# One transformer-like program on one core: four pieces of work put in another order on ScalarE and VectorE

## The chip, the core and the metric

The program runs on one core of one Trainium2 chip. Its engines work side by side, each on its own list of instructions, and wait for each other on semaphores: TensorE (PE) multiplies matrices, VectorE (DVE) and ScalarE (ACT) work element by element, SyncE (SP) starts the transfers from memory. The metric is the device time of one execution in microseconds (us). Shorter is better.

## The reference, cut to what matters

Two blocks follow each other on 256 tokens of width 1024, all in float32. The first has a modulated norm, a gated linear attention with a pooling branch, and 32 experts of which each token uses two. The second is where most of the change lies:

```
h = h + 0.5 * swiglu(rms_norm(h, ffn1_norm), ...)
u = rms_norm(h, mix_norm);  z = u @ w_in
(aq, ak, av, iq, ik, iw, rq, rk, rv, rg, ga, gb) = split(z)
aq, ak, iq, ik, rq, rk = rope(...)                       # rotation by position
y_a = dsa_attention(aq, ak, av, iq, ik, iw, n_sel=64)    # 64 best keys of an index score, then softmax
y_r = group_norm_heads(retention(rq, rk, rv), ret_gn) * silu(rg)
h = h + (sigmoid(ga) * (y_a @ w_branch_a) + sigmoid(gb) * (y_r @ w_branch_b)) @ w_out
h = h + 0.5 * swiglu(rms_norm(h, ffn2_norm), ...)
gate = sigmoid(rms_norm(h, ple_norm) @ w_ple_gate);  h = h + gate * (p @ w_ple_proj)
```

Of the first block the change touches the norm `x * rsqrt(mean(x*x) + 1e-6)` at its very start, beside the modulation `silu(c) @ w_ada`.

## The kernel before

Activations lie feature by token: a tile has 128 features on the partitions and 256 tokens beside each other, 8 tiles for the width. Weights come in chunks of 1 MB (128 x 2048), one DMA each, issued by SyncE into a ring of `raw` buffers; a buffer is loaded again when its last reader has given it back. Every product of an activation with a weight is made of three matmuls (`mm3`): both sides are split into a high part in a rounded format (`wh`, `hh`, `yh`) and a low part that holds the rest (`wl`, `hl`, `yl`). For the weights ACT copies half a chunk into `wh` (L1253, 128x1024) and DVE subtracts that from `raw` into `wl` (L1828). There are six slots of each, so both engines can be some halves ahead of PE. `ahead(name, i)` splits up to two chunks behind the named one, `through(name, i)` up to it, `done(...)` waits until PE has used it.

No scheduler orders the work. `tensor_program`, `scalar_program` and `vector_program` are written out by hand, and each engine runs its list in that order. A wait holds up everything behind it on its engine. PSUM has eight banks, given out to named jobs in the order of the PE list; `evicted(name)` waits until a bank has been read.

Four places matter:

- The start (ACT, L1296 to L1312). ACT squares the 8 tiles of `x` (L1299) for PE, which sums them with a matrix of ones; `root("statx", ...)` takes the square root, for which ACT must load another function table. `ada_row(1)` copies a row of `silu(c) @ w_ada` out of PSUM once PE has made it. Then come the squares of the context (L1309), which PE sums next. VectorE inverts the root (L1852), scales `x` and then the context, and both engines form the first inputs of the matmuls with `w1ak` (L1322 to L1328).
- The index queries (ACT L1669 to L1675, DVE L2468 to L2474). `shifted` copies the halves that the rotation swaps (L1601), `rope_rest` does the rotation (L2383 to L2389). PE is busy there with `w2rq`.
- The selection (DVE, `pick`, L2410 and L2492 to L2501). Eight rounds, in each of which for both halves of the queries the eight largest scores are found (L2413) and struck out (L2414). In between lie the splits for the weights `w2rv` and what follows, and `ret_scores(h)` (L2424), which multiplies the retention scores by their decays; PE's `ret_values(h)` waits for it.
- The four gates `rg` of the retention and the softmax of the attention (ACT L1711 to L1729, DVE L2517 to L2530). For each h there are `ahead("w2rg", h)`; for h = 0 and 1 the variance and mean of the last group norms (`ret_var`, `ret_mean`); the gate (`Silu`, and the product L2527, split by L1728 and L1848); and `attention(h)`. On DVE `attention(n)` masks and scales the logits (L2452), takes their maximum (L2455) and negates it (L2456), waits for ACT's two exponentials (L1659), and divides by the sum (L2458, L2460). `Sqrt`, `Silu` and `Exp` each need their own table on ACT. PE works in this order: `rg` h, then for n = h the transposes of softmax n-1 (L1106, `att_turn`, waits for L2460) and the logits of n (`att_probs`); at odd n from 3 on the attention values of two earlier ones go ahead (`att_values`). The same goes on for n = 4 to 7 beside `w2ga`.

Of the kernel before, what the change touches and what calls it, by code (L numbers as in the profile page):

```python
# [61 lines left out]
def program(nc, D, out):  # L62
# [8 lines left out]
    with cx:  # L71
# [16 lines left out]
        def S(name):  # L88
            return sems[name]

        def nth(name, n):
            return sems[name], base[name] + n
# [1146 lines left out]
        def scalar_program(a):  # L1239
# [56 lines left out]
            for k in range(8):  # L1296
# [2 lines left out]
                a.activation(SQ[k % 2][:, :], XT[:, k, :], ACT.Square).then_inc(S("sqx"), 1)  # L1299
                if k == 3:  # L1300
                    ada_row(0)
            ada_row(1)
            a.wait_ge(*nth("eps", 2))
            root("statx", "sqx_used", 8)
            a.wait_ge(*nth("d_ct", 16))
            for k in range(8):
                if k >= 2:
# [358 lines left out]
            for k in range(8):  # L1666
                a.wait_ge(*nth("hn_t", k + 1))
                a.activation(H1[:, k, :], TN[k % 2][:, :], ACT.Copy).then_inc(S("hn_h"), 1)
            through("w2rq", 0)  # L1669
            evicted(a, ("iq", 0))  # L1670
            shifted(0, TR[0], 2, 0)
            through("w2rq", 1)
            evicted(a, ("iq", 1))
            shifted(1, TR[1], 2, 0)
            rope_in_twice(2, "ik", ("w2ik", 0), TR[0], 8)  # L1675
# [35 lines left out]
            for h in range(4):  # L1711
                lin("w2rg", h)
                if h == 0:
                    ret_var(2)
                    ret_mean(3)
                    v2 = bank("av")[:, 0:128].rearrange("p (a c) -> p a c", a=2)
                    a.wait_ge(*nth("av_t", 1))
                    a.activation(AV[:, :, 0:64], v2, ACT.Copy)
                    copy_out("av", AV[:, :, 64:128], v2)
                elif h == 1:  # L1720
                    ret_var(3)
                if h < 2:
                    a.wait_ge(*nth("rope", 9 + h))
                else:
                    a.wait_ge(*nth("sgy", h - 1))
                copy_out(("rg", h), TR[h % 2], two(bank(("rg", h))), ACT.Silu)
                a.wait_ge(*nth("sgy", h + 1))
                a.activation(YH[:, 2 * h:2 * h + 2, :], YN[:, 2 * h:2 * h + 2, :], ACT.Copy).then_inc(S("rg_h"), 1)  # L1728
                attention(h)  # L1729
            for j in range(4):  # L1730
                lin("w2ga", j)
                a.wait_ge(*nth("rv_mm", 4))
# [83 lines left out]
        def vector_program(v):  # L1816
# [621 lines left out]
            def attention(n):  # L2438
# [6 lines left out]
                        t = v.tensor_tensor(YLA[p, hp, :], b[p, s * 256:s * 256 + 256], YHA[p, hp, :].bitcast(f32), ALU.subtract)  # L2445
                    t.then_inc(copied(("atv", hp)), 1)
                if n < 8:
                    a, P, M, Z = n % 2, P2[n % 2], NM[n % 2], SS[n % 2]
                    v.wait_ge(*nth("at_mm", 2 * n + 2))
                    if n >= 2:  # L2450
                        v.wait_ge(*nth("at_tr", n - 1))
                    v.scalar_tensor_tensor(P, two(bank(("atp", n))), 0.125, MB[:, a, :].unsqueeze(1).broadcast_to([128, 2, 256]), ALU.mult,  # L2452
                                           ALU.add).then_inc(copied(("atp", n)), 1)
                    evicted(v, ("atp", n))
                    chain(v.tensor_reduce(M[:, 0:2].unsqueeze(2), P, AX.X, ALU.max))  # L2455
                    v.tensor_scalar(M[:, 2:4], M[:, 0:2], -1.0, None, ALU.mult).then_inc(S("at_m"), 1)  # L2456
                    v.wait_ge(*nth("at_e", 2 * n + 2))
                    chain(v.reciprocal(Z[:, 2:4], Z[:, 0:2]))  # L2458
                    for s in range(2):
                        t = v.tensor_scalar(P[:, s, :], P[:, s, :], Z[:, 2 + s:3 + s], None, ALU.mult)  # L2460
                    t.then_inc(S("at_d"), 1)
# [6 lines left out]
            through("w2rq", 0)  # L2468
            rope_scaled(0, ("iq", 0), ("w2iq", 0), TR[0])
            rope_scaled(1, ("iq", 1), ("w2iq", 1), TR[1])  # L2470
            rope_rest(0, ("iq", 0), TR[0], 2, 0, IQ[:, 0:2, :])
            through("w2rq", 1)
            rope_rest(1, ("iq", 1), TR[1], 2, 0, IQ[:, 2:4, :])
            rope_rest(2, "ik", TR[0], 1, 0, IK.unsqueeze(1))  # L2474
            through("w2rk", 0)
# [13 lines left out]
            for p0, p1, a, c in ((0, 64, 0, 64), (64, 128, 0, 128), (0, 64, 1, 192)):  # L2489
                step(v.memset(SCO[p0:p1, a, c:256], -1e30))  # L2490
            prev()
            pick(0, 2)  # L2492
            ahead("w2rv", 0)
            pick(2, 4)
            ahead("w2rv", 1)
            ret_scores(0)
            pick(4, 6)
            ahead("w2rv", 2)
            ret_scores(1)
            pick(6, 8)  # L2500
            v.tensor_scalar(MB, WK, -3e38, -1e30, ALU.is_gt, ALU.mult).then_inc(S("ix_sel"), 1)  # L2501
            ahead("w2rv", 3)
            ret_mean(0)
            ret_scores(2)
            ahead("w2aq", 0)
            ret_var(0)
            ret_mean(1)
# [8 lines left out]
            v.wait_ge(*nth("ix_sel", 1))  # L2516
            for h in range(4):  # L2517
                ahead("w2rg", h)
                if h == 0:
                    ret_var(2)  # L2520
                    ret_mean(3)
                elif h == 1:
                    ret_var(3)
                Y2 = YN[:, 2 * h:2 * h + 2, :]
                evicted(v, ("rg", h))
                v.wait_ge(*nth("yn", h + 1))
                v.tensor_tensor(Y2, Y2, TR[h % 2], ALU.mult).then_inc(S("sgy"), 1)  # L2527
                v.wait_ge(*nth("rg_h", h + 1))
                low(YL[:, 2 * h:2 * h + 2, :], Y2, YH[:, 2 * h:2 * h + 2, :], "rg_l")
                attention(h)  # L2530
            for j in range(4):
                ahead("w2ga", j)
                attention(4 + j)
            for n, j in MERGE:
                ahead(n, j)
                if n == "w2gb" and j < 2:
# [276 lines left out]
```

## Time and profile before

| | us |
|---|---|
| median of 3 runs | 1164.95 |
| lowest and highest | 1160.52, 1165.49 |
| profiled execution, its own time | 1163.78 |
| its span | 1161.9 |
| PE busy (share of the span) | 1108.9 (95%) |
| DVE busy | 708.9 (61%) |
| ACT busy | 519.0 (45%) |

The span is the time from the first to the last instruction in the trace; 1.9 us of the execution lie around it. A busy PE is not a PE at its peak: the granted clock of TensorE has two levels, 1.2 and 2.4 GHz, and is shown as 0.5 and 1.0 of full speed; its mean over the span is 0.982. In the timeline a row gives the start in us from the span's start, the time it took, engine, line, operation, tile out of tile in, the count, and in brackets the idle time ahead of it with what ended it.

### The profile page before, as it was taken

How to read it: one execution, taken by the hardware profiler on the slowest of the kernel's cores; microseconds unless marked ns; L12 is line 12 of the kernel's file. 1: busy time of each engine (PE TensorE's matmuls, PEld its weight loads, DVE VectorE, ACT ScalarE, POOL GpSimd, SP SyncE). 2: the span in 40 equal slices, each digit the busy share in tenths (PEclk: the TensorE clock that was granted, in tenths of full speed). 3: DMA queues.
4: the chain of work that ended last, by engine and by line, in shares of the span. 5: the costliest groups of instructions: out<-in, count | busy, mean ns of one | idle time of the engine just before them, and what ended most of it. 6: DMA issues, size and time to landing. Idle time of an engine off the chain costs nothing.

```text
span 1161.9 us, 19096 instructions
## 1 busy us (share of the span) xinstructions
PE 1108.9 (95%) x7978; PEld 942.7 (81%) x7978; DVE 708.9 (61%) x1125; ACT 519.0 (45%) x797; POOL 0.2 (0%) x4
## 2 busy tenths in 40 slices
PE   5999999899999999999999999989999999999997
PEld 3789888545555554999999988987889999999997
DVE  1889868423332334786865689877646775655567
ACT  2773333211111113754444576368844554443455
POOL 0000000000000000000000000000000000000000
PEclk9999999899999999999999999998999999999998
DMA  9955627999999947465554423532246545445321
GB/s 384 357 190 215 245 78 294 382 421 421 417 403 409 411 195 321 144 242 188 208 183 156 180 84 118 181 109 91 92 145 227 182 182 207 184 153 217 127 94 37
DMA packets 38154, 257.74 MB, mean 222 GB/s; under 512 B 4368, under 2 KB 5264, under 8 KB 7856
## 3 DMA queue, kind: packets, MB, share of 16 engines
q1 hardware_dynamic: 36720, 252.38, 56.6%
q10 hardware_dynamic: 1344, 4.08, 0.9%
q8 instruction: 66, 1.08, 0.4%
q14 instruction: 24, 0.20, 0.0%
HBM read 255.39 MB, written 1.05 MB: 221 GB/s over the span
## 4 chain that ended last, share of the span: by engine, by line
PE 71%; DVE 9%; ACT 3%; issue 2%; DVEq 0%; ACTq 0%
PE bank L536 70%; DVE wl L1828 2%; ACT wh L1253 1%; DVE xt L1878 1%; DVE rstd L1852 1%; DVE hl L1895 1%; PE bank L922 0%; DVE acc L1890 0%; PE bank L1106 0%; PE bank L880 0%; DVE tn L1910 0%; DVE arena L2046 0%; ACT arena L1601 0%; DVE acc L2085 0%; DVE raw L1867 0%
## 5 line engine op out<-in xcount | busy, mean ns | idle before, releaser
L536 PE MATMUL bank<-hh,wh 128*128 128x256 f32 (+2 forms) x1256 | 364.3, 290 | 5.4 <-DVE wl L1828 3.4
L536 PE MATMUL bank<-hl,wh 128*128 128x256 f32 (+2 forms) x1256 | 360.0, 287 | 0.0
L536 PE MATMUL bank<-hh,wl 128*128 128x256 f32 (+2 forms) x1256 | 359.9, 287 | 0.0
L1828 DVE TENSOR_TENSOR wl<-raw,wh 128x1024 fp32r<-128x1024 f32 (+4 forms) x238 | 267.7, 1164 | 80.6 <-ACT wh L1253 76.8
L1253 ACT ACTIVATE wh<-raw 128x1024 fp32r<-128x1024 f32 (+4 forms) x238 | 227.9, 1003 | 71.4 <-PE bank L536 71.2
L536 PEld LDWEIGHTS bank<-hh,wh 128*128 128x128 f32 (+1 forms) x1256 | 242.5, 193 | 14.2 <-issue 9.5
L536 PEld LDWEIGHTS bank<-hl,wh 128*128 128x128 f32 (+1 forms) x1256 | 242.5, 193 | 1.0
L536 PEld LDWEIGHTS bank<-hh,wl 128*128 128x128 f32 (+1 forms) x1256 | 242.5, 193 | 0.9
L536 PE MATMUL bank<-yh,wh 128*128 128x256 f32 x512 | 146.6, 286 | 2.2 <-DVE yl L2445 1.7
L536 PE MATMUL bank<-yl,wh 128*128 128x256 f32 x512 | 145.4, 284 | 0.0
L536 PE MATMUL bank<-yh,wl 128*128 128x256 f32 x512 | 145.4, 284 | 0.0
L536 PEld LDWEIGHTS bank<-yh,wh 128*128 128x128 f32 x512 | 98.5, 192 | 3.7 <-issue 2.6
L536 PE MATMUL bank<-arena 64*128 64x256 f32 (+6 forms) x404 | 92.8, 408 | 6.5 <-DVE arena L2142 3.3
L536 PEld LDWEIGHTS bank<-yl,wh 128*128 128x128 f32 x512 | 98.7, 193 | 0.3 <-issue 0.2
L536 PEld LDWEIGHTS bank<-yh,wl 128*128 128x128 f32 x512 | 98.7, 193 | 0.0
L536 PE MATMUL bank<-raw,xg 128*64 128x512 f32 (+1 forms) x352 | 82.5, 567 | 0.1
L536 PEld LDWEIGHTS bank<-arena 64*128 64x128 f32 (+3 forms) x404 | 53.8, 181 | 32.1 <-issue 18.6
L2221 DVE SCALAR_TENSOR_TENSOR arena<-arena,bank 128x256 f32<-128x256 f32 x16 | 7.7, 481 | 106.1 <-ACT arena L1484 106.1
L1263 ACT ACTIVATE arena<-bank 128x512 f32<-128x512 f32 (+4 forms) x79 | 40.4, 532 | 69.3 <-PE bank L536 65.0
L536 PEld LDWEIGHTS bank<-raw,xg 128*64 128x64 f32 (+1 forms) x352 | 28.0, 142 | 45.6 <-issue 45.3
L1484 ACT ACTIVATE arena<-bank 128x256 f32<-128x256 f32 x16 | 6.1, 384 | 108.7 <-PE bank L536 108.7
L536 PE MATMUL bank<-raw,arena 128*64 128x512 f32 (+1 forms) x240 | 50.4, 549 | 1.1 <-DVE yl L2212 1.1
(275 smaller groups left out, 1405.1 us busy)
## 6 DMA issues: line engine op xcount, KB each, us to landing
raw<-in_gu SPq DMA_DIRECT2D x40, 1024.0 KB, 11.4
arena<-in_gu SPq DMA_DIRECT2D x24, 1024.0 KB, 10.4
raw<-in_gd SPq DMA_DIRECT2D x22, 1024.0 KB, 9.0
raw<-in_w_adt SPq DMA_DIRECT2D x14, 1024.0 KB, 6.1
raw<-in_f1g SPq DMA_DIRECT2D x11, 1024.0 KB, 4.8
raw<-in_f1d SPq DMA_DIRECT2D x11, 1024.0 KB, 5.5
raw<-in_f2g SPq DMA_DIRECT2D x11, 1024.0 KB, 4.9
raw<-in_f2u SPq DMA_DIRECT2D x11, 1024.0 KB, 4.9
```

What stands on the lines that cost most here:

```text
L536: return pe.matmul(o, l, m, start=start, stop=stop, skip_group_check=True)
L1253: a.activation(WH[slot_of[U]][:, 0:n], src, ACT.Copy).then_inc(S("wh"), 1)
L1263: a.activation(dst, src, fn).then_inc(copied(name), 1)
L1484: a.activation(SLT[p % 2], bank(("gu", p))[:, 0:256], ACT.Silu).then_inc(S("g_s"), 1)
L1828: v.tensor_tensor(WL[slot_of[U]][:, 0:n], src, WH[slot_of[U]][:, 0:n].bitcast(f32), ALU.subtract).then_inc(S("wl"), 1)
L1852: step(v.reciprocal(RS[:, :], RS[:, :]))
L1878: t = v.scalar_tensor_tensor(XT[:, k, :], b, s, XT[:, k, :], ALU.mult, ALU.add)
L1895: v.scalar_tensor_tensor(L[:, k, :], XT[:, k, :], gain[:, k:k + 1], H[:, k, :].bitcast(f32), ALU.mult, ALU.subtract).then_inc(S(sem), 1)
L2221: v.scalar_tensor_tensor(HSL[p % 2], SLT[p % 2], GC[:, p:p + 1], bank(("gu", p))[:, 256:512], ALU.mult, ALU.mult).then_inc(copied(("gu", p ...
```

## The change

Nothing is added or removed; instructions are put in another order on ACT and DVE. PE's, SyncE's and GpSimd's lists stay as they are.

- Start: `root("statx", ...)` goes ahead of `ada_row(1)` on ACT.
- Index queries: both splits for `w2rq` chunk 1 go ahead, on ACT ahead of the first `shifted`, on DVE ahead of the first `rope_rest`.
- Selection: the rounds, in portions of 2, 2, 2 and 2 between the splits before, are now taken in portions of 1, 2, 2, 1 and 2; the last two rounds and the mask `MB` come behind `ret_mean(0)` and `ret_scores(2)`.
- Gates: on ACT `attention(h)` goes ahead of the gate's `Silu`, and `ret_mean(3)` behind `attention(0)`. On DVE `attention(h)` is cut in two. The first part (mask, maximum, negation) goes ahead of `ret_var` and `ret_mean`, the second (`attention_scaled`: reciprocal and product) ahead of the gate's product.

```diff
@@ scalar_program
-            ada_row(1)
             a.wait_ge(*nth("eps", 2))
             root("statx", "sqx_used", 8)
+            ada_row(1)
@@
             through("w2rq", 0)
+            through("w2rq", 1)
             evicted(a, ("iq", 0))
             shifted(0, TR[0], 2, 0)
-            through("w2rq", 1)
             evicted(a, ("iq", 1))
@@
                 if h == 0:
                     ret_var(2)
-                    ret_mean(3)
                     v2 = bank("av")[:, 0:128].rearrange("p (a c) -> p a c", a=2)
...
                 elif h == 1:
                     ret_var(3)
+                attention(h)
+                if h == 0:
+                    ret_mean(3)
...
                 a.activation(YH[:, 2 * h:2 * h + 2, :], YN[:, 2 * h:2 * h + 2, :], ACT.Copy).then_inc(S("rg_h"), 1)
-                attention(h)
@@ vector_program
                     v.tensor_scalar(M[:, 2:4], M[:, 0:2], -1.0, None, ALU.mult).then_inc(S("at_m"), 1)
+
+            def attention_scaled(n):
+                if n < 8:
+                    P, Z = P2[n % 2], SS[n % 2]
                     v.wait_ge(*nth("at_e", 2 * n + 2))
                     chain(v.reciprocal(Z[:, 2:4], Z[:, 0:2]))
...
             rope_scaled(1, ("iq", 1), ("w2iq", 1), TR[1])
+            through("w2rq", 1)
             rope_rest(0, ("iq", 0), TR[0], 2, 0, IQ[:, 0:2, :])
-            through("w2rq", 1)
@@
-            pick(0, 2)
+            pick(0, 1)
             ahead("w2rv", 0)
-            pick(2, 4)
+            pick(1, 3)
             ahead("w2rv", 1)
             ret_scores(0)
-            pick(4, 6)
+            pick(3, 5)
             ahead("w2rv", 2)
             ret_scores(1)
-            pick(6, 8)
-            v.tensor_scalar(MB, WK, -3e38, -1e30, ALU.is_gt, ALU.mult).then_inc(S("ix_sel"), 1)
+            pick(5, 6)
             ahead("w2rv", 3)
             ret_mean(0)
             ret_scores(2)
+            pick(6, 8)
+            v.tensor_scalar(MB, WK, -3e38, -1e30, ALU.is_gt, ALU.mult).then_inc(S("ix_sel"), 1)
@@
             for h in range(4):
                 ahead("w2rg", h)
+                attention(h)
                 if h == 0:
                     ret_var(2)
                     ret_mean(3)
                 elif h == 1:
                     ret_var(3)
+                attention_scaled(h)
...
-                attention(h)
             for j in range(4):
                 ahead("w2ga", j)
                 attention(4 + j)
+                attention_scaled(4 + j)
```

The start, on ACT, as one piece of the difference; `sq<-xt` are the squares of x, `row` is what `ada_row` writes, `rstd` the root, `sq<-arena` the squares of the context:

```order
 L1263 ACTIVATE row<-bank 128x256
 L1299 ACTIVATE sq<-xt 128x256 x4
+L1267 ACT_TABLE_LOAD
+L1267 ACTIVATE rstd<-bank,small 128x256
 L1263 ACTIVATE row<-bank 128x256
-L1267 ACT_TABLE_LOAD
-L1267 ACTIVATE rstd<-bank,small 128x256
 L1309 ACTIVATE sq<-arena 128x256 x8
```

The second row copy now stands behind the table load and the root; the squares of the context follow it directly.

The selection, on DVE, before, from the last filling of masked scores (L2490) to the first split; a `MAX` with its `MATCH_REPLACE` is one half of a round, `wl<-raw,wh` a split:

```order
L2490 MEMSET arena 64x64
L2413 MAX small<-arena 128x8
L2414 MATCH_REPLACE arena<-small,arena 128x256
L2413 MAX small<-arena 128x8
L2414 MATCH_REPLACE arena<-small,arena 128x256
L2413 MAX small<-arena 128x8
L2414 MATCH_REPLACE arena<-small,arena 128x256
L2413 MAX small<-arena 128x8
L2414 MATCH_REPLACE arena<-small,arena 128x256
L1828 TENSOR_TENSOR wl<-raw,wh 128x1024 x2
```

and in the changed kernel:

```order
L2495 MEMSET arena 64x64
L2414 MAX small<-arena 128x8
L2415 MATCH_REPLACE arena<-small,arena 128x256
L2414 MAX small<-arena 128x8
L2415 MATCH_REPLACE arena<-small,arena 128x256
L1829 TENSOR_TENSOR wl<-raw,wh 128x1024 x2
```

One round stands ahead of the first split where two stood. From there to `ret_scores(0)` both lists read the same (two rounds and another split), so that three rounds lie ahead of it in place of four.

The first gate, on DVE, before (L1852 and L2435 are `ret_var(2)`, L2429 `ret_mean(3)`, L2527 and L1848 the gate's product and its low part, L2452 to L2460 the softmax):

```order
L1828 TENSOR_TENSOR wl<-raw,wh 128x1024 x2
L1852 RECIPROCAL rstd<-rstd 128x256
L2435 SCALAR_TENSOR_TENSOR arena<-arena,par,rstd 128x256 x2
L2429 SCALAR_TENSOR_TENSOR arena<-bank,arena 128x512
L2527 TENSOR_TENSOR arena<-arena 128x512
L1848 TENSOR_TENSOR yl<-arena,yh 128x512
L2452 SCALAR_TENSOR_TENSOR arena<-bank,arena 128x512
L2455 TENSOR_REDUCE small<-arena 128x2
L2456 TENSOR_SCALAR small<-small 128x2
L2458 RECIPROCAL small<-small 128x2
L2460 TENSOR_SCALAR arena<-arena,small 128x256 x2
```

and in the changed kernel:

```order
L1829 TENSOR_TENSOR wl<-raw,wh 128x1024 x2
L2453 SCALAR_TENSOR_TENSOR arena<-bank,arena 128x512
L2456 TENSOR_REDUCE small<-arena 128x2
L2457 TENSOR_SCALAR small<-small 128x2
L1853 RECIPROCAL rstd<-rstd 128x256
L2436 SCALAR_TENSOR_TENSOR arena<-arena,par,rstd 128x256 x2
L2430 SCALAR_TENSOR_TENSOR arena<-bank,arena 128x512
L2463 RECIPROCAL small<-small 128x2
L2465 TENSOR_SCALAR arena<-arena,small 128x256 x2
L2535 TENSOR_TENSOR arena<-arena 128x512
L1849 TENSOR_TENSOR yl<-arena,yh 128x512
```

The softmax's first part moved to the front, the group norm's rows lie between its two parts, and the gate's product is last. On ACT the row of exponentials with its table load moves ahead of the `Silu` with its own in the same way; there are 36 table loads in the list before and 36 in the list after.

## Rows read from the trace of the kernel before

**Rows 1.** The page's busy times, and share of the span.

```profile
PE 1108.9 (95%) x7978; PEld 942.7 (81%) x7978; DVE 708.9 (61%) x1125; ACT 519.0 (45%) x797; POOL 0.2 (0%) x4
```

**Rows 2.** Waits of PE, in 0:110, 660:745, 780:835 (total, times, longest us).

```profile
PE bank L536 <- ACT sq L1309: 2.1, 1, 2.1
...
PE bank L536 <- issue: 1.8, 1, 1.8
...
PE bank L1106 <- DVE arena L2460: 5.9, 1, 5.9
```

**Rows 3.** Timeline of ACT at the start.

```profile
21.64 0.85 ACT L1299 ACTIVATE sq<-xt 128x256 f32<-128x256 f32 x2 [0.35 <-PE bank L536]
25.17 0.38 ACT L1263 ACTIVATE row<-bank 128x256 f32<-128x256 f32 x1 [2.68 <-PE bank L536]
25.57 1.28 ACT L1267 ACT_TABLE_LOAD   x1
...
27.23 0.71 ACT L1309 ACTIVATE sq<-arena 128x256 f32<-128x256 f32 x2
```

**Rows 4.** Stretches: us, PE busy; of all engines where shown, then PEclk, DMA share, GB/s.

```profile
28.00:31.50 3.50, 3.50 (x10) 0.51 1.00 415
...
787.00:796.00 9.00, 8.94 (x34) 0.50 0.35 117
...
200.00:210.00 10.00, 6.70 (x53) 6.28 (x52) 7.63 (x34) 6.37 (x13) 0.00 (x0) 0.95 0.69 248
...
240.00:300.00 60.00, 60.00 (x340) 30.65 (x339) 18.38 (x37) 9.92 (x20) 0.00 (x0) 1.00 1.01 421
```

**Rows 5.** Timeline of DVE, first round's start, a later one, and ret_scores(0).

```profile
720.47 0.43 DVE L2413 MAX8 small<-arena 128x8 f32<-128x256 f32 x1
...
722.44 0.43 DVE L2413 MAX8 small<-arena 128x8 f32<-128x256 f32 x1
...
732.89 0.55 DVE L2424 TENSOR_TENSOR arena<-bank,arena 128x384 f32<-128x384 f32 x1
```

**Rows 6.** Timeline of ACT, the split for w2rv, chunk 0.

```profile
704.57 2.01 ACT L1253 ACTIVATE wh<-raw 128x1024 fp32r<-128x1024 f32 x2
```

**Rows 7.** Timeline of DVE around the first gates.

```profile
774.94 1.75 DVE L1852 RECIPROCAL rstd<-rstd 128x256 f32<-128x256 f32 x1
...
777.52 0.69 DVE L2429 SCALAR_TENSOR_TENSOR arena<-bank,arena 128x512 f32<-128x512 f32 x1
...
783.23 0.68 DVE L2452 SCALAR_TENSOR_TENSOR arena<-bank,arena 128x512 f32<-128x512 f32 x1
...
784.67 0.17 DVE L2456 TENSOR_SCALAR small<-small 128x2 f32<-128x2 f32 x1
786.00 0.17 DVE L2458 RECIPROCAL small<-small 128x2 f32<-128x2 f32 x1 [1.16 <-ACT arena L1659]
...
786.94 2.36 DVE L1828 TENSOR_TENSOR wl<-raw,wh 128x1024 fp32r<-128x1024 f32 x2
```

**Rows 8.** Timeline of ACT around the first gates.

```profile
778.24 0.72 ACT L1633 ACTIVATE sq<-arena 128x256 f32<-128x256 f32 x2 [4.37 <-DVE arena L2429]
...
780.61 0.60 ACT L1263 ACTIVATE arena<-bank 128x512 f32<-128x512 f32 x1
781.96 0.63 ACT L1728 ACTIVATE yh<-arena 128x512 fp32r<-128x512 f32 x1 [0.76 <-DVE arena L2527]
```

**Rows 9.** The chain that ended last, PE's transposes (start, us, what).

```profile
786.96 1.09 PE bank L1106 x4
...
798.91 0.44 PE bank L1106 x4
...
808.38 0.44 PE bank L1106 x4
...
816.15 0.51 PE bank L1106 x4
...
850.74 0.44 PE bank L1106 x4
```

More of the change, by code:

```diff
@@ L2447, in attention @@
                 if n < 8:
-                    a, P, M, Z = n % 2, P2[n % 2], NM[n % 2], SS[n % 2]
+                    a, P, M = n % 2, P2[n % 2], NM[n % 2]
                     v.wait_ge(*nth("at_mm", 2 * n + 2))
```

## The prediction

> **What bounds the kernel now.** The page's busy times come first [rows 1]: PE is busy for 95% of the span, DVE for 61%, ACT for 45%. So only PE's idle time, and what its clock loses behind it, can be won. Next the waits of PE in the stretches that the change touches [rows 2]. The reader is to see three: 2.1 us at the start, behind ACT's squares of the context; 1.8 us in the selection, put down to "issue"; and 5.9 us, the largest, at the transposes of softmax 0, behind DVE's L2460. Third come the timelines of DVE and ACT there, to see what stood ahead of the releaser in its list. In the selection the 1.8 us end with ret_scores(0) [rows 5]. Last, the stretches with the granted clock [rows 4]: it is at the lower of its two levels (0.5, 1.2 GHz) from 28.0 to 31.5 and again from 787 to 796, both times behind a PE that had waited. In the chain of waits [rows 9] two transposes with that stretch between them are 11.95 us apart (786.96 to 798.91), the same work at 2.4 GHz 7.77 us (808.38 to 816.15): 4.18 us for the clock. The step from 798.91 to 808.38, 9.47 us, holds a pair of attention values besides. These two, 7.77 and 9.47, are PE's pace per head, in turns.
>
> **Start (ACT).** Nothing is removed. Before, the squares of x end at 22.49 (21.64 + 0.85), ACT waits 2.68 us for PE's rows, copies one at 25.17, loads the table for 1.28 us, takes the root, and begins with the context at 27.23 [rows 3]. Now load and root stand ahead of the copy: 22.49 + 1.28 + 0.38 (27.23 less 26.85) = 24.15, inside the old wait. PE has the sum ready: in its list it stands ahead of the rows for which the copy waited until 25.17. The copy stays at 25.17 and the context begins at 25.57: 1.66 us earlier. PE's wait of 2.06 shrinks by it. Everything up to the first product with w1ak is a chain from these squares (squares, split, reciprocal, scaled context, modulation), so it moves by 1.66. DVE's reciprocal starts 3 us earlier and is not in its way. The clock's low stretch at 28.0 may fall away with the wait and give 0.6 more, if the squares then run at the pace of those of x; I take nothing for it. Does it reach the end? The experts stream at 421 GB/s, the transfers busy for 1.01 of the time, and bound the middle [rows 4]; but from 200 to 210 they are busy for only 0.69, so the buffers are full by then and the stream goes on when PE frees the first: it moves with PE. Range 0 to -2.3, taken -1.7.
>
> At this place the table load can be weighed. The trace has 1.28 us for it and the root right behind it, without a pause [rows 3]. The Trainium skill (ScalarE: Activation LUTs, What ACT_TABLE_LOAD costs) counts about 1283 ns for the load and 1380 ns of drain besides, 2.66 us at each change of set. By the page load and root would end at 25.5, behind the time of the copy, and this term would be about 1.3 in place of 1.7. The row decides; loads are 36 before and after.
>
> **Index queries.** From the first product with w2rq on PE does not wait until the selection [rows 2], so no wait is there to be taken away. The rotations may end some 2 us earlier. But DVE then comes to the split of w2rv, chunk 0, whose first half ACT delivers at 704.57 + 1.06 = 705.63, bound there by PE's own w2rk [rows 6], and DVE had been there at that moment anyway. So the lead ends before the selection: 0. It is 1.0 better at most, if the clock is not low under w2rq, and 0.5 worse if the first rotation then held back PE; taken 0.
>
> **Selection (DVE).** A round takes 722.44 - 720.47 = 1.97 us [rows 5]. With three ahead of it, ret_scores(0) starts at 732.89 - 1.97 = 730.92 and is done at 731.5, ahead of PE, which gets there at 731.6 to 731.8. The wait of 1.8 goes, and with the matmuls' overlap PE gains 1.95 (its next start was 733.55, now 731.60). What is late next? ret_scores(1) would be done at 738.2; PE wants it after w2rv 3 and a mean, at 740.3. The split of kv comes 3 us earlier than before. ret_scores(2) now waits for PE, until 742.3, then two rounds and the mask run to 747.1; ACT wants the mask for ret_values(2) at 753.5, and the split for w2aq 1, behind them in DVE's list, is done at 749.4 where PE starts on it at 754.5. So the nearest of these has 2 us of cover and the split 5 (read from the timelines of PE and ACT around 740 to 755, each less the 1.95; no term rests on them), and from 749 on DVE and ACT hang on PE's results. Range -1.95 to 0, taken -1.9.
>
> **Gates.** Times of before, all of which move by the same 1.9. DVE is free at 774.94 [rows 7]; PE's logits of softmax 0 are there at 774.3. Mask, maximum and negation take 784.67 + 0.17 - 783.23 = 1.61: 776.55. ACT loads its table meanwhile and needs about 1.15 from there: 777.7. On DVE ret_var(2) takes 777.52 - 774.94 = 2.58 and ret_mean(3) 0.6: 779.75. The second part takes 786.96 - 786.00, 0.9 without the signal: 780.6. PE's transposes, at 786.96 before, were ready to start at 786.96 - 5.86 = 781.1. The wait of 5.9 goes, and the low clock behind it with its 4.18 too. But that is not won. ACT squares for the mean (0.7) only after 779.8, then loads `Silu` (1.3) and applies it (0.6, [rows 8]): 782.4. Product 0.7, ACT's copy 0.65: 783.8. Then ACT's split, first half 1.06, DVE's split 2.3 [rows 7], first part 1.6, ret_var(3) 2.6, second part 0.9: 792.2. PE comes to the transposes of softmax 1 at 781.1 + 7.77 = 788.9, so a new wait of 3.3 us opens. From there a round of DVE and ACT is e to e: load 1.3, Silu 0.6, product 0.7, copy 0.65, split 1.06 + 2.3, first part 1.6, exponentials 1.1, handovers 0.2: 9.5, with attention values 10.2. Added up the softmaxes are done at 792.2, 800.8, 811.0, 821.0, 829.3; PE's transposes follow at 792.4, 801.9, 811.1 (a wait of 1.5), 821.1 (0.6), 829.4 (0.5), and then at PE's pace 838.9 and 846.6. Before, the last stood at 850.74 [rows 9]. So the term is 846.6 - 850.7 = -4.1, not -10. Behind it nothing is changed: the values of the last pair and the branches. Ends: -10.1 if DVE and ACT keep up with PE (5.9 + 4.2), and 0 if the new wait costs as much as the old one; my value is the chain's.
>
> **Sum.** -1.7 + 0 - 1.9 - 4.1 = -7.7. The profiled execution took 1163.78 (span 1161.9): 1156.1. The median of the three runs is 1164.95, from where it is 1157.2. I say 1156.6.
>
> **Rivals.**
> 1. The new wait pulls the clock down. For: 5.9 us of waiting did, and so did about 2 us at the start [rows 4]. Against: the 1.8 us of the selection did not. Price: one head at 1.2 GHz, +4.18, of which the waits of 1.5, 0.6 and 0.5 behind it take up 2.6: -2.5 in place of -4.1, total 1158.2. The Trainium skill (TensorE: Matmul & The Clock Gate, What's actually happening) has it that half rate is the default and that activity lifts it; by that rule the 3.3 us idle PE is in danger. The rows at 787 agree.
> 2. The start's gain is lost on the way, since it has to pass 800 us and the experts' stream. For: the stream is bound by transfers for 200 us. Against: the slack at 200. Total -6.0: 1158.3.
> 3. Slower. In place of one long wait there are four within 40 us (3.3, 1.5, 0.6, 0.5). If the low clock that the first brings stays through four heads, because PE never works without a break, they cost 4 x 4.18 = 16.7, less 2.6: -7.7 + 14.1 = +6.4, 1170. It decides from three heads on (-7.7 + 12.5 - 2.6 = +2.2). Against: before, the clock was back at 796 within one head.
> 4. The change doesn't do what it says: ret_scores(0) is done only 0.1 to 0.3 us ahead of PE, and the softmax 0.5 us ahead. If either is late by that much it costs just those tenths, so this is in the range and not beside it.
>
> **How the numbers follow.** Forecast 0.56; rival 1 0.17; rival 2 0.16; rival 3 0.05; the first two together (-4.4, 1159.5) 0.06. What a measurement here can tell from no change is about 0.5%, 5.8 us. The forecast lies 1.9 beyond that and gives 0.50 to faster, 0.06 to the same; rivals 1 and 2 (about -6) share half and half: 0.17 each way; the pair goes to the same. Faster 0.67, same 0.28, slower 0.05. The three runs of before lie 5 us apart, so the range runs from 1151.5 (start at -2.3, the low stretch under w2rq gone, the run at the low end) to 1162.0.
>
> **What would show it.** Right: no wait at L1106 near 780; a new one of about 3 us one head later, behind L2465, and small ones after; transposes of softmax 7 some 7.7 us earlier in the span; no wait at ret_values(0); ACT's context squares near 25.6; no gain between the first rotation and the selection. Wrong: a PE that waits for the split of w2aq 1 or for the mask; the clock low for more than one head behind 790; a first expert matmul that has not moved.

## The result, and the profile after

| | before | after |
|---|---|---|
| median (5 runs of each), us | 1163.79 | 1154.03 |
| lowest and highest | 1160.52, 1165.49 | 1149.88, 1155.87 |
| profiled execution (span) | 1163.78 (1161.9) | 1154.77 (1152.7) |
| mean granted clock of the profiled one | 0.982 | 0.984 |

The ratio of the times is 0.9913, 95% interval 0.9893 to 0.9934: 10.1 us faster (7.7 to 12.5). The prediction was 1156.6, 1151.5 to 1162.0, with 7.7 us of gain. The work is the same, only idle time and clock differ. The page's busy times after the change, beside [rows 1]:

```profile
PE 1107.5 (96%) x7978; PEld 941.2 (82%) x7978; DVE 708.5 (61%) x1125; ACT 519.4 (45%) x797; POOL 0.2 (0%) x4
```

PE's waits in the changed kernel, where [rows 2] had 2.1, 1.8 and 5.9 (total us, times, longest us). The first fence is of the stretch from 0 to 110 us, the second of 770 to 835; from 660 to 745 the row of 1.8 behind "issue" is gone:

```profile
PE bank L536 <- ACT sq L1309: 0.3, 1, 0.3
```

```profile
PE bank L1106 <- DVE arena L2465: 2.0, 2, 1.6
PE bank L1106 <- issue: 1.1, 1, 1.1
```

The start on ACT (start, us it took, what), the answer to [rows 3]. The load waits 0.83 us for PE's sum instead of standing right behind the squares, as I had it. The root lies in the copy's old wait all the same, and the squares of the context begin at 25.23:

```profile
21.41 0.85 ACT L1299 ACTIVATE sq<-xt 128x256 f32<-128x256 f32 x2 [0.36 <-PE bank L536]
23.09 1.28 ACT L1267 ACT_TABLE_LOAD   x1 [0.83 <-PE bank L536]
24.39 0.47 ACT L1267 ACTIVATE rstd<-bank,small 128x256 f32<-128x256 f32 x1
24.95 0.38 ACT L1263 ACTIVATE row<-bank 128x256 f32<-128x256 f32 x1
25.23 0.71 ACT L1309 ACTIVATE sq<-arena 128x256 f32<-128x256 f32 x2
```

The selection on DVE [rows 5]: the first round's start and `ret_scores(0)` are 10.45 us apart where they were 12.42 (732.89 - 720.47), one round of 1.97 less:

```profile
717.67 0.43 DVE L2414 MAX8 small<-arena 128x8 f32<-128x256 f32 x1
...
728.12 0.55 DVE L2425 TENSOR_TENSOR arena<-bank,arena 128x384 f32<-128x384 f32 x1
```

The first two gates on DVE [rows 7] and on ACT [rows 8]. Softmax 0 ends with DVE's L2465 at 775.07, softmax 1 with the one at 786.56. The `Silu` of head 0 is ACT's L1263 at 777.02:

```profile
775.07 0.62 DVE L2465 TENSOR_SCALAR arena<-arena,small 128x256 f32<-128x256 f32 x2
777.65 0.69 DVE L2535 TENSOR_TENSOR arena<-arena 128x512 f32<-128x512 f32 x1 [1.97 <-ACT arena L1263]
...
783.78 1.75 DVE L1853 RECIPROCAL rstd<-rstd 128x256 f32<-128x256 f32 x1
785.57 0.88 DVE L2436 SCALAR_TENSOR_TENSOR arena<-arena,par,rstd 128x256 f32<-128x256 f32 x2
...
786.56 0.61 DVE L2465 TENSOR_SCALAR arena<-arena,small 128x256 f32<-128x256 f32 x2
```

```profile
774.99 0.72 ACT L1633 ACTIVATE sq<-arena 128x256 f32<-128x256 f32 x2 [2.08 <-DVE arena L2430]
775.73 1.28 ACT L1263 ACT_TABLE_LOAD   x1
777.02 0.60 ACT L1263 ACTIVATE arena<-bank 128x512 f32<-128x512 f32 x1
```

And PE's transposes, the first two in the timeline, the last in the chain [rows 9]:

```profile
777.72 0.63 PE L1106 MATMUL bank<-csts,arena 128*128 128x128 f32 x4 [1.07 <-issue]
...
787.32 0.63 PE L1106 MATMUL bank<-csts,arena 128*128 128x128 f32 x4 [1.64 <-DVE arena L2465]
```

```profile
841.28 0.44 PE bank L1106 x4
```

Where the time went can be read from the place of PE's instructions, each compared with the same instruction in before. They stand 3.1 us earlier at 42 us (first product with `w1ak`), 2.9 at 218, 1.3 at 660, 2.8 at 692 (behind `w2rq`, where before had a stretch of low clock), 4.8 at 733 (selection), 9.2 at the first transposes and 9.5 from the fifth on. So this pair shows 1.3 us for all that lies ahead of 660, 1.5 under `w2rq`, 2.0 for the selection and 4.7 for the gates. The experiments show which of these belong to the edits.

### The profile page after: what moved, and what is told of

The parts are those of the page before. It is cut to its first block, busy times and chain, and to the rows that moved or that the text cites. A ratio compares the mean times of both kernels' runs of the same rounds, so it can differ in the third digit from the quotient of the medians.

```text
span 1152.7 us, 19097 instructions
## 1 busy us (share of the span) xinstructions
PE 1107.5 (96%) x7978; PEld 941.2 (82%) x7978; DVE 708.5 (61%) x1125; ACT 519.4 (45%) x797; POOL 0.2 (0%) x4
## 4 chain that ended last, share of the span: by engine, by line
PE 68%; DVE 10%; ACT 5%; issue 2%; DVEq 0%; ACTq 0%
PE bank L536 67%; DVE wl L1829 3%; ACT wh L1253 2%; DVE xt L1879 1%; DVE rstd L1853 1%; ACT L1263 1%; DVE hl L1896 1%; PE bank L922 0%; DVE acc L1891 0%; ACT arena L1263 0%; ACT arena L1659 0%; PE bank L880 0%; DVE tn L1911 0%; DVE arena L2047 0%; DVE arena L2535 0%
## 5 line engine op out<-in xcount | busy, mean ns | idle before, releaser
L1263 ACT ACTIVATE arena<-bank 128x512 f32<-128x512 f32 (+4 forms) x79 | 40.4, 532 | 73.3 <-PE bank L536 69.0
```

The lines of the kernel that those rows point to most:

```text
L1263: a.activation(dst, src, fn).then_inc(copied(name), 1)
```

## The experiments

All times are medians; every group of runs had its runs of the kernel before on the same chip.

| kernel | us | ratio to before, 95% |
|---|---|---|
| start alone | 1157.48 | 0.9948 (0.9934 to 0.9962) |
| index queries alone | 1162.49 | 0.9987 (0.9974 to 1.0) |
| selection alone | 1161.01 | 0.9970 (0.9958 to 0.9983) |
| gates alone | 1159.46 | 0.9958 (0.9944 to 0.9972) |
| changed kernel again | 1152.77 | 0.9917 (0.9900 to 0.9935) |
| changed, without the start edit | 1155.80 | 0.9933 (0.9919 to 0.9947) |
| changed, new order in head 0 only | 1157.57 | 0.9954 (0.9939 to 0.9969) |
| changed, first Silu earlier (two series) | 1149.60, 1148.81 | 0.9877 (0.9856 to 0.9899), 0.9877 (0.9860 to 0.9895) |
| the same, and variance 3 later | 1154.22 | 0.9924 (0.9907 to 0.9941) |
| before, gates' wait filled | 1164.70 | 1.0014 (1.0001 to 1.0026) |
| before, start's wait filled | 1161.15 | 0.9982 (0.9970 to 0.9994) |

**The four parts, one each** (its hunk of the diff above, on the kernel before). Start:

> The kernel before with the first edit alone (the norm's root on ScalarE ahead of the row copy). Theory A: the first product of the context's sum waits for the squares of the context, which now follow the root; in the changed kernel that product was at 25.69 us instead of 27.70, and the wait of TensorE ahead of it fell from 2.06 to 0.27 us. Alone it should do the same (2.0 earlier), carry 1.3 to 3.1 us into the experts' stream and end 1.3 to 3.1 us below the kernel before. Rival (start's gain is lost): the product is earlier, but the stretch of low clock in the first 220 us falls elsewhere, and the first expert product is less than 0.5 us earlier; the time is within 0.5 us of before.

Measured: 6.0 us faster by the ratio (4.4 to 7.7), far more than the trace shows at the edit's own place (1.8 us, see the start below). Index queries:

> The kernel before with the fourth edit alone (VectorE's two halves of iq ahead of the rotation of the first two heads, TensorE's w2rq half in the same order). Theory A: no wait of TensorE ends on it, 0 +-0.3 us. Rival: in the changed kernel the granted clock was not low under w2rq (690.11 - 678.45 = 11.66 us from the selection's products to it, against 13.17 before), so if the edit itself keeps the clock high this kernel is 1.5 us faster and shows full clock at 680 to 684. If theory A is right, the clock at 680 is low here too, or is high in before-like kernels at random, and the median shows under 0.6 us.

Measured: 1.5, interval 0 to 3.0. Its trace has full clock at 680, and PE's waits from 660 to 745 as before, the 1.8 among them:

```profile
680.00:690.00 10.00, 10.00 (x86) 10.00 (x85) 8.91 (x14) 9.58 (x18) 0.00 (x0) 1.00 0.61 211
```

But so have the kernels with the start or the gates alone, which don't have this edit, while two kernels that have it (the first Silu earlier, and that with the variance later, both below) were low from 677 to 681. So the full clock is not the edit's. What this trace gained at 680 by the clock it had lost at 470, where before was not low; the changed kernel lost there too:

```profile
470.00:480.00 10.00, 8.54 (x59) 8.57 (x60) 8.38 (x17) 7.93 (x16) 0.00 (x0) 0.83 0.52 174
```

The edit has a worth of its own all the same, and it shows only where the clock is full under `w2rq`. There, PE comes to chunk 1 earlier, and in the old order it waits 1.0 us for VectorE's split, which stands behind the first rotation. The trace of the start alone has that wait, and two waits for such splits from 660 to 745:

```profile
680.11 0.36 PE L536 MATMUL bank<-hh,wh 128*128 128x256 f32 x1 [0.99 <-DVE wl L1828]
```

```profile
PE bank L536 <- DVE wl L1828: 2.3, 2, 1.3
```

The trace of this edit alone has one:

```profile
PE bank L536 <- DVE wl L1828: 1.3, 1, 1.3
```

Ten of the fourteen traces have full clock there. From the place of 680 us in before to that of 692, the four of them without the edit are 0.29 or 0.30 us shorter than before, and the six with it 1.50 or 1.51. The four traces with the low clock, two with the edit and two without, lie within 0.1 of each other. So theory A (0 within 0.3) holds at the low clock alone: at full clock the edit gives 1.2 us, and it gives them in the changed kernel. Selection:

> The kernel before with the third edit alone (selection rounds in portions of 1, 2, 2, 1, 2). Theory A: TensorE's wait of 1.8 us for the first head's scores of retention goes (in the changed kernel it was 0), and nothing later waits for the later rounds: 1.9 us faster (-1.7 to -2.0). The gates follow 1.9 us earlier as a block. Rival: in the gates the softmaxes and TensorE stand in one chain through VectorE, and VectorE's gates start no earlier than the last selection round ends, so that half of it is given back in the first wait at the gates: -0.9 us.

Measured: 3.5 by the ratio (2.0 to 4.9); PE's place moves by 1.96 to 1.98 between 725 and 735 us in all eight traces that have the edit, and here it keeps that through the gates. The rival with half given back falls. Gates:

> The kernel before with the second edit alone (softmax ahead of the retention's gate in each round, on ScalarE and VectorE). In the changed kernel the gates' stretch, from the wait at 750 to the eighth head's turn, took 4.7 us less (before 749.92 to 850.58, after 745.15 to 841.12). Theory A: the edit removes the wait of 5.86 us ahead of the first transposes and leaves 1.6 us at the second, with 0.3 at the fifth, and nothing at the others: -4.0 to -4.7 us alone. Rival B: part of the 4.7 us is the granted clock (10.2 us at the low level in before at 786, 3.4 in after at 800), which goes by the length of the wait and not by the order; then this kernel shows the same clock as the changed one. Rival C: the gain rests on the selection's edit too (VectorE is free 1.9 us later here, relative to TensorE), and alone it is -2.5 to -3.

Measured: 4.9 by the ratio, and 4.71 in the trace from 763 to 861 us, against 4.69 in the changed kernel. PE's waits there are those of the changed kernel within a tenth:

```profile
PE bank L1106 <- DVE arena L2465: 2.0, 2, 1.7
PE bank L1106 <- issue: 1.1, 1, 1.1
```

So the selection's edit is not needed for it: rival C falls. Of rival B the next runs tell.

**The changed kernel again.**

> The changed kernel once more, beside the parts. The parts alone gave -6.0 (start), -2.5 (selection), -4.1 (gates) and -1.0 (iq) by medians, -13.6 together, where the changed kernel had -9.8 by its medians. Theory A: the parts add up, and what lacks is the low clock between 120 and 220 us, which differs from one execution to the next in identical code (the traces of the changed kernel and of the kernel with the start edit alone are the same program up to 660 us, yet stand 5.4 us apart at 218): 1150 to 1154 here, with a profile whose clock below 220 us may differ from the first. Rival: the start edit's gain and the others' overlap; then again 1154 +-1 and the same stretches of low clock.

Measured: 1152.77. Its profile is 5.5 us ahead of the first one of the same program at 218 us and 5.3 at 660. Of the 5.5 it has 0.8 already at 24.3 us, ahead of any low clock; 3.1 are clock, since the first profile was low at 130 to 137 us and the second not; and 1.5 come between 160 and 180 us, where both lost the same 1.7 us to the clock but only the first has waits (0.9 us) as well. The low stretch in the granted clock (the columns behind the engines are granted clock, DMA share, GB/s):

```profile
130.00:140.00 10.00, 10.00 (x47) 8.26 (x46) 4.31 (x12) 2.27 (x3) 0.00 (x0) 0.66 0.56 210
```

```profile
130.00:140.00 10.00, 10.00 (x69) 8.48 (x68) 6.55 (x14) 2.78 (x4) 0.00 (x0) 1.00 0.50 203
```

Up to 218 us it is the trace of the start edit alone to 0.1 us. Every trace has some such stretches; each loses 1.7 us of full clock, or 3.4 or 5.1 where it is two or three times as long, and where they fall changes between executions of one program.

**The wait of 1.07 us** at the first transposes, which the prediction did not have and the view puts down to "issue": on ACT the first `Silu` ahead of the squares of `ret_mean(3)`.

```diff
                 attention(h)
-                if h == 0:
-                    ret_mean(3)
                 if h < 2:
                     a.wait_ge(*nth("rope", 9 + h))
...
                 copy_out(("rg", h), TR[h % 2], two(bank(("rg", h))), ACT.Silu)
+                if h == 0:
+                    ret_mean(3)
```

> The changed kernel, with ScalarE's Silu of the first retention gate ahead of the squares of the fourth head's mean. Theory A: TensorE's remaining wait of 1.07 us at the first transposes is a wait for their bank (seven banks in a ring, and the first transposes take the bank that held the first gate's product), which that Silu frees at 777.02 + 0.60 = 777.62 us, 0.10 before the transposes start at 777.72. ScalarE had stood 2.08 us ahead of the squares, so the Silu with its table load (1.88 us) fits in: wait 1.07 gone or under 0.2, the rest of the round 0.9 to 1.1 us earlier, -1.0 us against the changed kernel. Rival: it is TensorE's own queue (the view names no releaser, only issue): the wait stays at 1.07 and the time is the same.

Measured: 1149.60 beside 1152.77. The wait is gone: the transposes start at 776.33, right behind the matmuls ahead of them (a matmul's end is modelled, here at 776.49). The bank had been free since 774.67, when the `Silu` ended:

```profile
776.33 0.49 PE L1106 MATMUL bank<-csts,arena 128*128 128x128 f32 x3
```

```profile
774.07 0.60 ACT L1263 ACTIVATE arena<-bank 128x512 f32<-128x512 f32 x1
774.83 0.72 ACT L1633 ACTIVATE sq<-arena 128x256 f32<-128x256 f32 x2 [0.16 <-DVE arena L2430]
```

So it was the bank. From 763 to 861 us the trace is 6.73 us shorter than before, 2.04 more than the changed kernel: 1.07 for the wait, some 1.5 for the clock, which was never low in the gates here, less 0.5 of waits behind DVE that grow (2.5 in sum for 2.0):

```profile
770.00:830.00 60.00, 57.09 (x404) 50.16 (x403) 44.40 (x76) 52.61 (x82) 0.00 (x0) 1.00 0.32 106
```

Once more, in another series:

> The version with the first Silu ahead of the squares once more, for the claim that it beats the changed kernel (1149.6 beside 1152.8 in the last comparison; 2.04 us less than it between 763 us and the end of the gates in the traces, of which 1.07 were the wait for the bank and the rest the clock, which was never low there). Expected: 1148 to 1152 again, the stretch from the third sum of the retention's mean to the last transposes the same within 0.2 us. Rival: the clock of the gates differs by itself too; then the stretch is 1 to 1.5 us longer than in the first trace.

Measured: 1148.81, the stretch 6.80, again never low. This version beats both kernels: over both series the median of 9 runs is 1148.81, of the changed kernel's 10 runs 1153.36.

**The variance of head 3 behind softmax 1** (`ret_var(3)` behind `attention(1)` on ACT, behind `attention_scaled(1)` on DVE), on top of it:

```diff
-                elif h == 1:
-                    ret_var(3)
                 attention(h)
+                if h == 1:
+                    ret_var(3)
```

> As v_silu, and the root, reciprocal and two products of the fourth head's variance behind the second softmax instead of ahead of it. Theory A: the wait of 1.64 us at the second transposes is the length of VectorE's reciprocal and two products (785.57 + 0.88 - 783.78 = 2.6 us) between the second softmax's maximum and its scaling, and of ScalarE's root with its load: without them the wait is 0, and nothing later waits for the fourth head's variance before 806 us: 1.6 us better than v_silu, 2.6 better than the changed kernel. [...]

Measured: 1154.22, 4.6 slower than without, and 2.9 in the trace's stretch. My expectation was wrong. The wait at the second transposes goes, but ACT now has a load and the root between the exponentials and the `Silu`, and VectorE takes its 2.6 us ahead of the gate's product:

```profile
782.64 1.28 ACT L1267 ACT_TABLE_LOAD   x1
783.93 0.47 ACT L1267 ACTIVATE rstd<-bank,small 128x256 f32<-128x256 f32 x1
784.42 1.28 ACT L1263 ACT_TABLE_LOAD   x1
785.72 0.60 ACT L1263 ACTIVATE arena<-bank 128x512 f32<-128x512 f32 x1
787.74 0.64 ACT L1730 ACTIVATE yh<-arena 128x512 fp32r<-128x512 f32 x1 [1.43 <-DVE arena L2535]
```

Ahead of softmax 1 the reciprocal and its products filled VectorE's wait for ACT's load and exponentials. Behind it, VectorE waits 1.16 us for the exponentials and 0.96 for the root, and the gate's product starts at 787.02 where it stood at 785.31 without the change. The waits come back as 1.3 and 2.2 at the third and fourth transposes, and the clock is low behind them:

```profile
PE bank L1106 <- DVE arena L2465: 3.5, 2, 2.2
PE bank L536 <- ACT arena L1263: 0.5, 1, 0.5
```

**The order of before with its wait filled**, by 13 products of 128x256 that nobody reads.

```diff
                 b = take(pe, ("att", n))
+                if n == 0:
+                    keep_clock(b, 13)
                 pe.wait_ge(*nth("at_d", n + 1))
```

> The kernel before, with 13 products that nobody reads put on TensorE into the transposes' bank within its wait of 5.86 us ahead of the first transposes. It leaves the order as before and takes away the idle stretch behind which the clock was at its low level for 10.2 us. Theory A: the softmaxes on VectorE and ScalarE set the round's pace, TensorE had 0 to 0.6 us of wait at the later transposes of before, and a faster TensorE waits there instead: within 1 us of before, with new waits of 3 to 4 us in sum at the second and third transposes. Rival B: the low clock was on the path (the round from the first to the second transposes took 11.79 us at the low clock, against 7.96 in the changed kernel without its wait): 3.8 us faster than before, and then most of the gates' 4.7 us could be had without a new order.

Measured: 1.0014, no gain, and 2.14 longer in the trace from 763 to 861 us. The clock is high where it was low [rows 4], but PE runs into a wait of 3.0 at the second transposes, and the low stretch comes behind that one:

```profile
786.00:796.00 10.00, 7.97 (x58) 6.83 (x56) 7.75 (x10) 7.99 (x13) 0.00 (x0) 1.00 0.29 106
796.00:804.00 8.00, 6.87 (x25) 5.20 (x26) 5.99 (x10) 6.70 (x10) 0.00 (x0) 0.57 0.38 130
```

Counted from 763 us, the second transposes come 0.7 us earlier than in before. So much had half clock behind the 5.9 us cost; the rest VectorE and ACT would have cost too, and the gain of the gates is the order's.

**The new order in the first head only** (for h = 1 to 3 the gate's `Silu`, product and splits ahead of the softmax, as before).

> The changed kernel, but with the gate ahead of the softmax again (the order of before) in the rounds of the second, third and fourth retention head; only the first head's round keeps the new order. Theory A: ScalarE and VectorE are one chain through all rounds, so the second softmax, which now stands behind the second gate's Silu, product, split and the weight split, comes 3 to 4 us later than 787.2: TensorE's wait at the second transposes grows from 1.64 to about 5, behind it the clock is low, and from there the pace is that of before: 3 to 4 us slower than the changed kernel, so that of the gates' 4.7 us about 1 is left. Rival: only the first wait (5.86) was on the path, before had no wait at the later transposes in the old order; then the time is that of the changed kernel, or better by the waits of 1.64 and 0.31.

Measured: 4.2 slower than the changed kernel's 10 runs by the medians, and 5.5 in the trace's stretch, which is 0.8 longer than that of before: nothing is left of the gain. The wait has moved by one head and the clock with it:

```profile
PE bank L1106 <- DVE arena L2467: 5.4, 1, 5.4
PE bank L1106 <- issue: 1.1, 1, 1.1
```

```profile
789.00:799.00 10.00, 9.94 (x44) 8.24 (x45) 7.41 (x12) 8.67 (x13) 0.00 (x0) 0.57 0.30 107
```

**The start.** Undone in the changed kernel:

> The changed kernel with the start's edit undone (row copy ahead of the root again). Five traces with that edit and five without it stand 2.9 us apart on the mean at 115 us (the first product of k's turn) and 4.0 at 660, where the prediction had 1.7 (up to 2.3). Theory A: the edit is worth the difference of these groups, 4 us on the mean, since VectorE's unbroken stretch from 67 to 100 us begins earlier with it: this kernel is 3 to 5 us slower than the changed one (1156 to 1158), and TensorE's wait ahead of w1q at about 100 us is 1.3 to 1.8 us long. Rival (the prediction's sum): 1.7 us slower, 1154.5.

Measured: 0.9933 against 0.9913 and 0.9917: about 2 us. That is nearer to the prediction's 1.7 than to the 4 of my theory, but the three intervals together leave about 2 us either way, so the times alone do not exclude 4. PE's wait ahead of `w1q` (the last row) is 0.3 although the edit is undone, so that this wait is not the edit's:

```profile
PE bank L536 <- ACT raw L1263: 2.9, 1, 2.9
PE bank L536 <- ACT sq L1309: 2.1, 1, 2.1
PE bank L536 <- DVE wl L1829: 0.3, 1, 0.3
```

And its wait filled, in the kernel before, by 7 such products:

```diff
             b = take(pe, "statc")
+            keep_clock(b, 7)
```

> The kernel before, with 7 products that nobody reads on TensorE in its wait of 2.06 us ahead of the context's sum; the order stays. Theory A: the first product still waits for the context's squares (27.2 to 27.7 us), but the clock stays high under the 16 products behind it, which take 4.7 us instead of 5.9 (in two of five traces of the old order the clock was low there, in three not): about 1.1 us where it was low, and nothing of the 2 us of the root's wait; 0 to -1.5 us in the median. What it can't give is VectorE's earlier start, so the wait at 102 stays. Rival: the start edit's whole gain is the clock; then this kernel has it too: -4 us or more.

Measured: 0.9982, 2.1 us (0.7 to 3.5). The clock was high, but the 7 products stand in the trace as 14 matmuls of 0.23 us and took 3.27 us in a gap of 2.06, so that the context's sum waited for them: the rows behind it are 0.3 us earlier than in before, not 1.1. The rival's 4 us lie outside the interval.

```profile
24.87 3.27 PE L536 MATMUL bank<-csts 128*128 128x256 f32 x14
```

All traces together tell the start's own size. From PE's product at 24.3 us, ahead of the context's sum, to the one at 33.4 behind it, the seven traces with the edit are 2.90 us shorter than before (+-0.02). Of the five other traces without the edit and without filling, two had the low clock at 28 us and are 0.02 and 0.17 longer, and three had not and are 1.11 shorter. So the edit gives 1.79, and 1.1 more where the clock would have been low, as it was in three of six traces of the old order, before's own included, and in none of seven of the new.

## Why the prediction was right, and where it was off

- **Start, -1.7.** Right in mechanism and size: 1.79, and with half of the clock's 1.1 about 2.3, my end of the range. I had put that part at 0.6 and counted nothing for it. The gain passes the experts' stream, as argued: PE stands 2.9 us ahead at 218 us and still 2.9 at 461. Rival 2 falls. The other part is the difference between the start edit alone, 6.0 faster, and its undoing, which cost 2. From 40 to 230 us the traces lose 6.8 to 10.2 us to the clock with the edit (mean 8.5 of seven) and 8.5 to 11.9 without (mean 10.2 of six, the filled start left out). The granted clock of every run, and not of the traced ones alone, says more. Time lost to the clock (the span times what its mean granted clock lacks to 1) was 22.1 us on the mean in the 18 runs of before beside the parts and 17.3 in the five of the start alone, 4.7 less; it was 16.5 in the ten of the changed kernel and 18.7 in the six with the start undone, 2.2 less. What is left of the span is 1.0 shorter with the edit both times (standard errors 0.6 and 0.7). So most of what the start gave alone came with less low clock, in four of its five runs. Why the clock was low less often, and less so in the changed kernel, stays open.
- **Index queries, 0.** Right for an execution with the low clock under `w2rq`, as before's trace has it, and wrong for the others: there the edit is worth 1.2. The step that failed is "no wait is there to be taken away", read from that one trace; with full clock the old order has a wait of 1.0. I had written "1.0 better at most, if the clock is not low under w2rq" and then taken 0, and "no gain between the first rotation and the selection" did not hold. The changed kernel's 1.5 there are 0.3 of clock and 1.2 of the edit.
- **Selection, -1.9.** Right: 1.96 to 1.98 in each trace. Nothing was late next.
- **Gates, -4.1.** Right in mechanism, measured -4.7. With the 4.77 us added back that PE was ahead by then, the end of softmax 1 is at 791.9 where I had 792.2, and the transposes are at 782.5, 792.1, 803.1, 810.9, 820.8, 828.6, 838.1 and 845.9, where the prediction had 792.4, 801.9, 811.1, 821.1, 829.4, 838.9 and 846.6 for the last seven. The next softmaxes end at 800.5, 810.7, 820.7 and 828.4, where it had 800.8, 811.0, 821.0 and 829.3 (these steps are not the 9.5 and 10.2 of its round alone, and it does not say how it came to them). The step that failed is the first: PE's transposes were not at 781.1. They waited for their own bank, which the `Silu` of head 0 gives back, and which the change puts behind `attention(0)` and the squares. I had listed what waits for the softmax and not what waits for the `Silu` that is moved, and "no wait at L1106 near 780" was wrong by 1.07 us. As VectorE and ACT set the pace, PE's being late by 1.4 shortened the wait behind it from 3.3 to 1.64. Of the waits of 1.5, 0.6 and 0.5 only 0.3 was left.
- **Rival 1** (low clock behind the new wait) did happen, in part: from 790 to 800 us the changed kernel has a granted clock of 0.89, and the step from the second to the third transposes took 11.02 for 9.47. The waits that I had counted behind it took that up. The Trainium skill (TensorE: Matmul & The Clock Gate, What's actually happening) has it that activity lifts the rate and its lack lets it fall; behind waits of 5.4 and 5.9 us the traces agree. Behind the waits of 1.7 to 2.1 us (at 28, at 470) the clock was low in some executions and not in others, and at 130 it was low in the changed kernel's first trace behind no wait of over 0.5 us.
- **Rival 3** (low through four heads) fell: 1.7 us lost to the clock in place of 16.7.
- **The sum.** With full clock under `w2rq`, 1.8 to 2.9, 1.2, 2.0 and 4.7 are 9.7 to 10.8, against 10.1 (7.7 to 12.5) and 9.7 measured. The forecast was 2.4 short, of which 1.2 is the index queries', 0.6 the gates' and 0.1 to 1.2 the start's. By the ratios the four parts give 15.9 when each is alone (6.0, 1.5, 3.5, 4.9), far more than together. In the runs' clocks, what the parts take off the span beside lost clock adds up (1.0, 1.2, 2.0 and 1.3, against 5.1 for the changed kernel; the standard error of each is 0.6 to 0.9), and the lost clock does not (4.7, 0.2, 0.8 and 3.0 against 5.5).

## What to carry to other kernels

Where two engines off the critical path feed the third in turns, price a move by the whole round of the two and not by the wait that it removes: 10 us of wait and clock (5.9 and 4.2) were worth 4.7, and filling the wait was worth nothing. For every instruction that moves back, list who waits for what it gives back, its bank above all; the view showed that wait only as "issue", and putting one `Silu` back ahead gave 2.0 us more in the trace and 4.5 by the medians. "PE does not wait here" is read from one execution: where that one had the low clock, another can have a wait, as `w2rq` has. Before one explains a difference of 1.7 or 3.4 us between two traces, one should take the same program's trace twice, and look at the granted clock of all runs.

## What the runs showed that I had not expected

- Two traces of one program differ by 5.5 us at 218 us (2.9 and 8.4 ahead of before), 3.1 of it by one low stretch of the clock. Lost time comes in portions of 1.7 us; the fourteen traces lose 12.9 to 21.0 us in the whole span, with no order that I can name.
- A load of the function table took 1.28 us everywhere, and the next instruction stood 0.01 us behind it wherever it did not have to wait for another engine. Copies and squares never had a load of their own: in the changed kernel a copy of 0.59 us stands between the root and the load for the exponentials.
- Waits of PE of about 2 us are followed by the low clock in some executions of a program and not in others: at 28 us in three of six traces of the old order, with the wait at 2.05 or 2.06 in all of them.
- The wait for a bank that ACT gives back was put down to "issue". What gave it away is that the transposes started 0.10 us behind the end of the `Silu`.
